# A two-block transformer kernel on one core: modulation sums turned outside the FFN loops, one sum for the final norm and the norm behind it, first chunks interleaved

## The chip, the cores and the metric

The kernel runs on one core of a Trainium2 chip. The time is the device time of one execution in microseconds (us), and before the change the median of three runs is 1651.37 us (1649.37 to 1656.2).

## What is computed

Two blocks work in a row on x, 256 tokens of width 1024, in f32. Each layer follows one pattern (shift, scale and gate come from the conditioning vector c):

```
mod = silu(c) @ mod_w[layer] + mod_b[layer]
h = rms_norm(x, norm_g) * (1 + sc1) + sh1
x = x + g1 * mixer(h)
h = rms_norm(x, norm_g) * (1 + sc2) + sh2
x = x + g2 * conv_ffn(h)
```

Block 1 has the mixers "state space + attention" (ab_in, glu, ab_out) and "conformer convolution" (cm_in, a gate, 31 causal taps per channel, a layer norm, silu, cm_out). It ends with `x = rms_norm(x, final_g)`. Block 2 has latent attention over x and a context ctx (dq, dkv, uq, ukv, 16 heads, mla_out) and a hyena mixer (hy_in, long filters, hy_out), and a final norm of its own. The FFN is 1024 to 2 x 2816 and back, with three taps per channel on the gate.

The change touches the place where the blocks meet. There the reference computes y = x * r * final_g with r = 1/sqrt(mean(x^2) + EPS), and then rms_norm(y, norm_mix_g_2).

## The kernel before

**Data.** Features lie on the 128 partitions, tokens in the free dimension: x is eight tiles of 128x256. Each f32 product is made as three products of rounded parts, hi*hi, lo*hi and hi*lo (`three`, L1845). So a chunk of weights (1 MB, 128x2048) costs 48 matmuls of 256 columns with eight feature tiles. Weights stream through three slots on SyncE's DMA queue; ScalarE makes w_hi (L650), VectorE w_lo (L1095). `chunk_ready` waits for both.

**Norms.** ScalarE squares x, two tiles at a time (L659). TensorE sums over the partitions with a matrix of ones (`norm_sum`, L1785: eight f32 matmuls, sixteen passes). ScalarE takes the root (L665), VectorE the reciprocal (`norm_rstd`, L1244). Then pair by pair of tiles: VectorE scales (L1262), ScalarE makes h_hi (L677), VectorE h_lo (L1272). `feature_chunk` and `up_gate` begin when the first pair is there, and go tile by tile of the output, each over all eight feature tiles. `final_norm` scales x in place (L1532).

**FFN.** `ffn` is a loop of five iterations of two steps on every engine. A step takes three chunks (gate, up, down); taps and silu run on VectorE and ScalarE (L1432).

**Modulation vectors.** mod_pe, for layer 0, goes over TensorE at the start. For both second layers the matrix mod_stream is multiplied on VectorE inside ffn0 and ffn1 (`mod_block`, L1123 to L1137, sixteen blocks of 384 columns each). `mod_turn` on TensorE (L1799, three matmuls of one column, six passes) sums a block's partitions, three times per iteration and once at the end. Products stand in a ring of three (`mod_acc`), for which `mod_block` waits. mod_later, for block 2's first layer, comes in 48 pieces of 512 KB into a ring of six slots, and TensorE multiplies them in rounds, `later(p)` (L2078), between the parts of the conformer stage; `later_copy` (ScalarE, L884) and `later_turn` (L2066) bring the results into columns.

**Conformer stage.** Eight chunks of cm_in, two a round. `conv_taps` (L2057) does 8 of the 31 taps on TensorE as products with diagonal matrices, VectorE the other 23 (L1574, 23 for each of the two tiles). The layer norm needs a sum of its own (L2094). The order is written out by hand:

```
for c in range(2 * p, 2 * p + 2):
    feature_chunk(Q["cm_in"] + c, ...)
if p:
    conv_taps(p - 1)
    later(p)
```

**Between the blocks.** final_norm(FINAL), then norm 6 of the scaled x, then the products dq and dkv with ctx's norm between them, then uq.

## Time and profile before

| | |
|---|---|
| median of three runs | 1651.37 us (1649.37 to 1656.2) |
| the profiled execution | 1647.83 us, its span 1646.0 us |
| mean granted TensorE clock | 0.956 |
| PE busy | 1495.4 us, 91% of the span |
| DVE (VectorE) busy | 1208.4 us, 73% |
| ACT (ScalarE) busy | 724.2 us, 44% |
| data read from HBM | 304.17 MB |

The span is one execution recorded on the core. PE is TensorE, SP SyncE, POOL GpSimd. The chain of waits follows the work that ended last back to the beginning: each row is a piece of an engine's work, or a transfer, that held up what came next. A row such as "PE bank L1845 x96" is 96 matmuls in one piece. The windows table gives what each engine was busy in a stretch of time, with the granted clock (1.00 is full).

### The profile page before, as it was taken

The numbers are of one execution on the slowest core, as the hardware profiler recorded it, in microseconds if no ns is written. First come the engines' busy times: TensorE is split into PE (matmuls) and PEld (weight loads), VectorE is DVE, ScalarE is ACT, GpSimd is POOL, SyncE is SP. The second block draws the span as 40 slices with busy tenths as digits, with TensorE's granted clock in tenths as the row PEclk, the third lists the DMA queues.
The fourth block names the chain that finished last, engine by engine and source line by source line (L and its number), as shares of the span: only waits on it lengthen the run. The fifth ranks groups of instructions, "written<-read, shape, count | busy, mean of one in ns | idle before, by whom it ended". The sixth has DMA issues, their size and how long they took to land.

```text
span 1646.0 us, 29088 instructions
## 1 busy us (share of the span) xinstructions
PE 1495.4 (91%) x11238; PEld 1348.5 (82%) x11238; DVE 1208.4 (73%) x1913; ACT 724.2 (44%) x949; POOL 52.1 (3%) x38
## 2 busy tenths in 40 slices
PE   4597898999989878999978899999999999899998
PEld 1484488999987668999967766889998877899997
DVE  7998647888879956888875545386666769466665
ACT  2222445444454235443444566354545442355443
POOL 2501200000000000000001000000000000000000
PEclk9698999999999989999979899999999999999999
DMA  8334827878845744878822400335554433245551
GB/s 350 128 103 166 298 99 301 316 297 309 325 163 197 275 193 184 347 294 304 301 111 103 128 14 1 130 106 202 178 185 170 164 119 103 77 149 176 182 182 51
DMA packets 55188, 307.85 MB, mean 187 GB/s; under 512 B 6631, under 2 KB 7688, under 8 KB 30984
## 3 DMA queue, kind: packets, MB, share of 16 engines
q1 hardware_dynamic: 53272, 302.40, 49.6%
q10 hardware_dynamic: 1840, 4.41, 0.9%
q8 instruction: 51, 0.84, 0.2%
q14 instruction: 25, 0.20, 0.0%
HBM read 304.17 MB, written 1.05 MB: 185 GB/s over the span
## 4 chain that ended last, share of the span: by engine, by line
PE 83%; DVE 9%; ACT 4%; issue 2%; DMA 2%; POOL 0%; ACTq 0%; DVEq 0%
PE bank L1845 66%; PE bank L1785 2%; PE bank L2192 2%; PE bank L2057 2%; PE bank L2042 2%; PE bank L2158 2%; DVE rstd L1244 2%; DMA arena<-in_mod_later 1%; DVE hf L1262 1%; DVE h_lo L1272 1%; PE bank L1799 1%; PE bank L2176 1%; PE bank L1811 1%; ACT w_hi L650 1%; PE bank L1896 1%
## 5 line engine op out<-in xcount | busy, mean ns | idle before, releaser
L1845 PE MATMUL bank<-h_hi,w_hi 128*128 128x256 f32 x2184 | 639.4, 293 | 64.1 <-DVE h_lo L1272 53.3
L1845 PE MATMUL bank<-h_lo,w_hi 128*128 128x256 f32 x2184 | 627.9, 287 | 0.0
L1845 PE MATMUL bank<-h_hi,w_lo 128*128 128x256 f32 x2184 | 627.4, 287 | 0.0
L1095 DVE TENSOR_TENSOR w_lo<-raw,w_hi 128x2048 fp32r<-128x2048 f32 x186 | 426.5, 2294 | 135.2 <-ACT w_hi L650 134.1
L1845 PEld LDWEIGHTS bank<-h_hi,w_hi 128*128 128x128 f32 x2184 | 428.5, 196 | 79.4 <-issue 65.8
L1845 PEld LDWEIGHTS bank<-h_lo,w_hi 128*128 128x128 f32 x2184 | 429.7, 197 | 1.1 <-issue 0.7
L1845 PEld LDWEIGHTS bank<-h_hi,w_lo 128*128 128x128 f32 x2184 | 428.9, 196 | 0.0
L650 ACT ACTIVATE w_hi<-raw 128x2048 fp32r<-128x2048 f32 x186 | 355.3, 1911 | 163.9 <-PE bank L1845 117.9
L1845 PE MATMUL bank<-a_hi,w_hi 128*128 128x256 f32 (+1 forms) x760 | 222.5, 293 | 9.9 <-DVE a_lo L1272 3.7
L1845 PE MATMUL bank<-a_lo,w_hi 128*128 128x256 f32 (+1 forms) x760 | 220.2, 290 | 0.0
L1845 PE MATMUL bank<-a_hi,w_lo 128*128 128x256 f32 (+1 forms) x760 | 220.0, 290 | 0.0
L1432 DVE SCALAR_TENSOR_TENSOR arena<-bank,par,arena 128x255 f32<-128x255 f32 (+1 forms) x264 | 109.1, 476 | 123.0 <-ACT arena L824 89.0
L1845 PEld LDWEIGHTS bank<-a_hi,w_hi 128*128 128x128 f32 x760 | 149.1, 196 | 12.7 <-DVE a_lo L1272 3.9
L1845 PEld LDWEIGHTS bank<-a_hi,w_lo 128*128 128x128 f32 x760 | 149.0, 196 | 0.8
L1845 PEld LDWEIGHTS bank<-a_lo,w_hi 128*128 128x128 f32 x760 | 149.0, 196 | 0.6
L824 ACT ACTIVATE arena<-bank,par 128x256 f32<-128x256 f32 x88 | 44.8, 560 | 170.5 <-PE bank L1845 170.5
L1129 DVE SCALAR_TENSOR_TENSOR arena<-arena,silu_c 128x384 f32<-128x384 f32 x192 | 104.3, 612 | 0.0
L1574 DVE SCALAR_TENSOR_TENSOR hf<-arena,par,hf 128x256 f32<-128x256 f32 x176 | 70.7, 480 | 1.0 <-DVE hf L1574 0.5
L1785 PE MATMUL bank<-sq,ones 128*128 128x256 f32 x208 | 53.8, 403 | 9.4 <-ACT sq L659 9.4
L842 ACT ACTIVATE a_hi<-arena 128x512 fp32r<-128x512 f32 x44 | 27.8, 631 | 67.5 <-DVE arena L1453 67.4
L1785 PEld LDWEIGHTS bank<-sq,ones 128*128 128x128 f32 x208 | 39.7, 201 | 17.3 <-ACT sq L659 12.0
L1244 DVE RECIPROCAL rstd<-std 128x256 f32<-128x256 f32 x15 | 26.3, 1752 | 37.2 <-ACT std L665 37.2
(265 smaller groups left out, 1486.6 us busy)
## 6 DMA issues: line engine op xcount, KB each, us to landing
raw<-in_stream SPq DMA_DIRECT2D x186, 1024.0 KB, 4.9
arena<-in_mod_stream SPq DMA_DIRECT2D x64, 768.0 KB, 6.4
arena<-in_mod_later SPq DMA_DIRECT2D x48, 512.0 KB, 6.8
raw<-in_mod_pe SPq DMA_DIRECT2D x36, 512.0 KB, 5.8
arena<-in_mod_pe SPq DMA_DIRECT2D x12, 512.0 KB, 12.6
sq<-in_bias SPq DMA_DIRECT2D x8, 256.0 KB, 7.0
x<-in_x_t ACTq DMA_DIRECT2D x1, 1024.0 KB, 9.2
arena<-in_ctx_t SPq DMA_DIRECT2D x1, 1024.0 KB, 4.9
```

The costliest lines, as they stand in the source:

```text
L650: nc.scalar.activation(w_hi[s][:], raw[s][:], ACT.Copy).then_inc(hi_done, 1)
L824: ins = nc.scalar.activation(gate_c[:, e, :], half(4, e), ACT.Identity, scale=par[:, bass.ds(wb[center] + 2 * s + e, 1)], bias=par[:, bass ...
L1095: nc.vector.tensor_tensor(w_lo[s][:], raw[s][:], w_hi[s][:].bitcast(F32), ALU.subtract).then_inc(lo_done, 1)
L1129: ins = nc.vector.scalar_tensor_tensor(acc[:, e, :], w, c, acc[:, e, :], ALU.mult, ALU.add)
L1244: nc.vector.reciprocal(rstd[:], std[:]).then_inc(sem("rstd_ready"), 1)
L1432: ins = nc.vector.scalar_tensor_tensor(o, src, par[:, bass.ds(w[tap] + 2 * s + e, 1)], o, ALU.mult, ALU.add)
L1574: chain.on(nc.vector.scalar_tensor_tensor(hf[:, k, :], padded[:, k, bass.ds(tap, T)], par[:, bass.ds(wt + k + DT * tap, 1)], hf[:, k, :], ...
L1785: ins = nc.tensor.matmul(bank[7][:, 0:T], ones[:], sq[:, k, :], start=(k == 0), stop=(k == 2 * pairs - 1))
L1845: ins = nc.tensor.matmul(out_, l, r, start=first and n == 0, stop=last and n == 2, **kw)
L2042: ins = nc.tensor.matmul(bank[2 * part + ft][:], dft[:, part, t, ft * P:(ft + 1) * P], sources[part][:, t, 512 * s_:512 * s_ + 512], start ...
L2057: nc.tensor.matmul(half(p % 3, e), diag[n], padded[:, 2 * p + e, t0:t0 + T], start=(t == 0), stop=(t == PE_TAPS - 1)).then_inc(sem("diag_u ...
L2158: nc.tensor.matmul(bank[u % 4][:], q_head[0:n, h, t * P:(t + 1) * P], k_head[0:n, h, :], start=True, stop=True)\
```

## The change

- mod_turn leaves the FFN loops. The sums of the sixteen blocks stay in `mod_keep`, so mod_block no longer waits for a ring. They are turned later: of ffn0's blocks 2 to 5 ahead of the last down product, 0 and 1 behind the sum of norm 2, 6 to 10 and 11 to 15 in the conformer stage; of ffn1's all between BOTH's sum and the k_pe turn. mod_out follows them.
- Ten taps on TensorE instead of eight (PE_TAPS).
- The pieces of mod_later per round are 0, 9, 9, 11, 11, 8 instead of 6, 8, 8, 8, 10, 8. The ring of six slots lies elsewhere, and its first six loads wait for all blocks of ffn0.
- FINAL and norm 6 become one norm, BOTH: the squares of x are scaled by both_q = sqrt(final_g^2 + EPS) and the sum takes EPS^2, the gain is the product of both gains. x itself is scaled after the uq product: four squares on ScalarE, a sum on TensorE and final_norm on VectorE; the addition of mla_out waits for it.
- Norm parts are made tile by tile, with three scaled ahead. The last two tiles of x are squared one by one.
- First chunks behind a norm take all their output tiles per pair of feature tiles (`feature_chunk` with staged, `first_up_gate`); their banks are opened with a product of zeros.
- `stay_awake(n)` issues n products of zeros (128x512, bf16) ahead of the first chunk: 13 in each FFN, 12 before cm_in, 20 before cm_out, 8 before dq, 17 before hy_in.

```diff
@@ -39,7 +39,7 @@
...
-PE_TAPS = 8
+PE_TAPS = 10
...
-        diag = [at(ffn0 + i * P, P) for i in range(2 * PE_TAPS)]
...
+        diag = [at(FREE - 2 * PE_TAPS * P + i * P, P) for i in range(2 * PE_TAPS)]
+        later_w = [at(i * PM_COLS, PM_COLS) for i in range(LATER_SLOTS)]
+        later_acc = [at(FREE + START_SLOTS * HALF + MOD_BLOCKS * MOD_COLS + (1 + i) * T, T) for i in range(2)]
+        MOD_KEEP = FREE + START_SLOTS * HALF
+        mod_keep = at(MOD_KEEP, MOD_BLOCKS * MOD_COLS)
...
         def later_pieces(p):
-            return range((0, 6, 14, 22, 30, 40)[p], (6, 14, 22, 30, 40, 48)[p])
+            return range((0, 0, 9, 18, 29, 40)[p], (0, 9, 18, 29, 40, 48)[p])
@@ -505,7 +507,9 @@
...
 
                 for m in range(m0, m1):
-                    if m >= LATER_SLOTS:
+                    if m < LATER_SLOTS:
+                        sp.wait_ge(sem("mod_used"), MOD_SLOTS + 2 * MOD_BLOCKS)
@@ -569,17 +573,15 @@
...
+            load_plain("cm_in", 0, 2)
             load_later(0, 6)
-            load_plain("cm_in", 0, 6)
-            load_later(6, 12)
-            load_plain("cm_in", 6, 7)
-            load_later(12, 18)
-            load_plain("cm_in", 7)
-            load_later(18, 20)
+            load_plain("cm_in", 2)
             load_plain("cm_out", 0, 1)
-            load_later(20, 27)
-            load_plain("cm_out", 1, 3)
-            load_later(27, 48)
+            load_later(6, 9)
+            load_plain("cm_out", 1, 2)
+            load_later(9, 15)
@@ -656,34 +659,48 @@
...
+            def square_tile(n, k):
+
+                by = both_q[:, k:k + 1] if n == BOTH else 1.0
+                nc.scalar.activation(sq[:, k, :], NORMS[n]["src"][:, k, :], ACT.Square, scale=by).then_inc(sem("sq_ready"), 1)
 
...
-                nc.scalar.activation(std[:], bank[7][:, 0:T], ACT.Sqrt, bias=eps[:, 0:1], scale=1.0 / NORMS[n]["width"])\
+                nc.scalar.activation(std[:], bank[7][:, 0:T], ACT.Sqrt, bias=(eps_2 if n == BOTH else eps)[:, 0:1], scale=1.0 / NORMS[n]["width"])\
...
-                    if ready is not None:
+                    if ready is not None and p == DT // 2 - 1:
+                        act.wait_ge(sem("x_half"), X_HALF[n])
+                        square_tile(n, DT - 2)
                         act.wait_ge(sem("x_ready"), ready + p + 1)
-                    square(n, p)
...
             norm_std(0)
+            act.wait_ge(sem("both_sum"), 1)
+            nc.scalar.activation(both_q[:], both_q[:], ACT.Sqrt).then_inc(sem("both_q_ready"), 1)
...
             ffn(1)
...
-
-            norm_x(6, 8)
...
+            for p in range(DT // 2):
+                square(FINAL, p)
+            norm_std(FINAL)
@@ -1100,17 +1126,16 @@
...
-                ring = mod_acc
-                acc = ring[b % len(ring)]
-                if b >= len(ring):
-                    dve.wait_ge(sem("mod_turned"), b - len(ring) + 1 + 3 * per)
+                part = mod_acc[b % len(mod_acc)]
+                k0 = b % MOD_BLOCKS * MOD_COLS
+                parts = [mod_keep[:, bass.ds(k0 + 3 * MOD_COLS * per, MOD_COLS)], part[:, 1, :]]
...
+            final_g = par[:, COL["final_g"]:COL["final_g"] + DT]
+            nc.vector.tensor_tensor(both_g[:], final_g, par[:, COL["norm_mix_g_2"]:COL["norm_mix_g_2"] + DT], ALU.mult)
+            link(nc.vector.tensor_tensor(both_q[:], final_g, final_g, ALU.mult))
+            nc.vector.tensor_scalar(both_q[:], both_q[:], EPS, None, ALU.add).then_inc(sem("both_sum"), 1)
@@ -1255,29 +1283,29 @@
...
+                tiles = v["kt"]
+
+                def scaled(k):
+                    nc.vector.scalar_tensor_tensor(hf[:, k, :], v["src"][:, k, :], gain(k), rstd[:], ALU.mult, ALU.mult)\
+                        .then_inc(sem("scaled"), 1)
+
...
+                    if k % 2:
+                        ins.then_inc(sem("h_ready"), 1)
+
+                for k in range(min(3, tiles)):
+                    scaled(k)
+                for k in range(tiles):
+                    lower(k)
+                    if k and k + 2 < tiles:
+                        scaled(k + 2)
@@ -1499,11 +1529,10 @@
...
-                if b0 is not None:
-                    mod_out((1, 4)[f], b0 + MOD_BLOCKS, ("mod_b", "mod_b_2")[f], 48)
...
+            mod_out(1, 6, "mod_b", 0, 18)
             norm(2)
...
                     add_taps(p - 1)
+                if p == 1:
+                    mod_out(1, 16, "mod_b", 18, 48, 2)
...
             ffn(1, 1, MB[4], 8)
-            final_norm(FINAL)
-
-
-            norm(6)
...
+            mod_out(4, 32, "mod_b_2")
@@ -1636,6 +1668,7 @@
...
+            final_norm(FINAL)
@@ -1673,6 +1706,7 @@
...
+            dve.wait_ge(sem("x_ready"), 12)
             add_to_x("mla_out", 3, 16)
...
             def norm_pair(n, p):
 
                 pairs = NORMS[n]["kt"] // 2
-                pe.wait_ge(sem("sq_ready"), SQ[n] + p + 1)
                 for k in range(2 * p, 2 * p + 2):
+                    pe.wait_ge(sem("sq_ready"), 2 * SQ[n] + k + 1)
                     ins = nc.tensor.matmul(bank[7][:, 0:T], ones[:], sq[:, k, :], start=(k == 0), stop=(k == 2 * pairs - 1))
                 if p == pairs - 1:
...
                     norm_pair(n, p)
 
-            def mod_turn(b, column, i=None, parts=2):
-
-                ring = mod_acc
-                pe.wait_ge(sem("mod_used"), MOD_SLOTS + 2 * b + 2 + (0 if i is None else 6 * i))
-                for n in range(3):
-                    for e in range(parts):
-                        ins = nc.tensor.matmul(bank[6][:, bass.ds(column + n, 1)], ring[b % len(ring)][:, e, n * P:(n + 1) * P], ones[:, 0:1],
-                                               start=(e == 0), stop=(e == parts - 1))
-                ins.then_inc(sem("mod_turned"), 1)
+            def stay_awake(n):
+
+                for i in range(n):
+                    nc.tensor.matmul(bank[i % 3][:], zeros[:, 0:P], zeros[:], start=True, stop=True)
+
+            def mod_turn(b0, blocks, dst=6):
+
+                for b in blocks:
+                    pe.wait_ge(sem("mod_used"), MOD_SLOTS + 2 * (b0 + b) + 2)
+                    for n in range(3 * b, 3 * b + 3):
+                        ins = nc.tensor.matmul(bank[dst][:, n:n + 1], mod_keep[:, n * P:(n + 1) * P], ones[:, 0:1], start=True, stop=True)
+                    ins.then_inc(sem("mod_turned"), 1)
 
...
+                    if late:
+                        pe.wait_ge(staged[0], staged[1][0])
+                    open_banks(fill, tiles // 2)
+                    for j, k in enumerate(order):
+                        if j % 2 == 0:
+                            pe.wait_ge(staged[0], staged[1][j // 2])
+                        for n in range(tiles):
+                            ins = three(half(4 + (fill + n // 2) % 2, n % 2), w_at(q, k, kt, n * P), (hh[:, k, :], hl[:, k, :]),
+                                        False, j == kt - 1, skip_group_check=True)
+                    ins.then_inc(chunk_done, 1)
+                    return
                 for n in range(tiles):
                     if n % 2 == 0 and fill + n // 2 >= 2:
                         pe.wait_ge(bank_free, fill + n // 2 - 1)
                     bb = 4 + (fill + n // 2) % 2
@@ -1981,24 +2035,45 @@
...
+            def ffn(f, b0=None):
...
+                stay_awake(13)
...
+                def first_up_gate(q, staged):
...
+                    def pair(j, n, p):
+                        for k in (2 * p, 2 * p + 1):
+                            ins = three(half(4 + j, n), w_at(q + j, k, DT, n * P), (h_hi[:, k, :], h_lo[:, k, :]), False, k == DT - 1,
+                                        skip_group_check=True)
+                        return ins
+
+                    for p in range(DT // 2):
+                        pe.wait_ge(staged[0], staged[1][p])
+                        pair(0, 0, p)
+                        ins = pair(0, 1, p)
+                        if p == DT // 2 - 1:
+                            ins.then_inc(chunk_done, 1)
+                        pair(1, 0, p)
+                    for p in range(DT // 2):
+                        ins = pair(1, 1, p)
+                    ins.then_inc(chunk_done, 1)
+
@@ -2016,21 +2091,17 @@
                             ins.then_inc(sem("down_done"), 1)
                     ins.then_inc(chunk_done, 1)
 
...
                         up_gate(s, q, i)
-                        if b0 is not None and e:
-                            mod_turn(b0 + 1, 9 * i + 3, i, parts=1)
                         down(s - 1, q + 2, i)
-                        if b0 is not None:
-                            mod_turn(b0 + 2 * e, 9 * i + 6 * e, i, parts=1)
+                if f == 0:
+                    mod_turn(b0, range(2, 6))
                 down(10, q0 + 32, last=True)
-                if b0 is not None:
-                    mod_turn(b0 + 15, 45, parts=1)
...
             norm_sum(2)
+            mod_turn(MB[1], (0, 1))
+            stay_awake(12)
...
                     conv_taps(p - 1)
+                if p < 2:
+                    mod_turn(MB[1], range(6 + 5 * p, 11 + 5 * p), 2)
+                if p:
...
             later(5)
             later_turn(5)
             norm_sum(LAYER_NORM)
+            stay_awake(20)
             projection("cm_out", 4, h_of(LAYER_NORM))
-            ffn(1, MB[4])
-            norm_sum(5)
-
-
-            norm_sum(6)
+            ffn(1)
+            norm_sum(BOTH)
+            mod_turn(MB[4], range(0, 3))
+            stay_awake(8)
             for c in range(2):
-                feature_chunk(Q["dq"] + c, FILL["dq"] + c, DT, h_hi, h_lo, staged=None if c else h_of(6))
+                feature_chunk(Q["dq"] + c, FILL["dq"] + c, DT, h_hi, h_lo, staged=None if c else h_of(BOTH))
                 if c == 0:
-                    norm_sum(7)
-            pe.wait_ge(sem("h_ready"), H[8])
+                    norm_sum(6)
+                    mod_turn(MB[4], range(3, 6))
+            mod_turn(MB[4], range(6, 11))
+            pe.wait_ge(sem("h_ready"), H[7])
...
                 if c == 0:
-                    norm_sum(8)
+                    norm_sum(7)
+                    mod_turn(MB[4], range(11, 14))
+            mod_turn(MB[4], range(14, 16))
...
-                    norm_sum(10)
+                    norm_sum(9)
+            norm_sum(FINAL)
...
             norm_sum(12)
+            stay_awake(17)
```

On TensorE, in the FFN loop (bank<-ones is mod_turn, a_hi,w_lo ends a down product, h_hi,w_hi begins gate or up), before:

```order
L1845 MATMUL bank<-a_hi,w_lo 128x256
L1796 REGISTER_ALU
L1799 ISA
L1799 MATMUL bank<-ones,arena 128x1
L1799 ISA
```

and after, at the end of the loop in ffn0:

```order
L1882 MATMUL bank<-a_hi,w_lo 128x256
L2097 REGISTER_ALU
L2097 COMPARE_AND_BRANCH
L1837 MATMUL bank<-ones,arena 128x1 x12
L1882 MATMUL bank<-a_hi,w_hi 128x256
```

No mod_turn is left inside; four blocks' stand behind it.

On TensorE, in the conformer stage, between the second and third pair of cm_in's chunks (L2057 and L2130 are taps, L2078 and L2151 pieces of mod_later, L2066 and L2139 later_turn), before:

```order
L1845 MATMUL bank<-h_hi,w_lo 128x256
L2057 MATMUL bank<-arena 128x256 x16
L2078 MATMUL bank<-arena 32x256 x8
L2066 MATMUL bank<-ident_sb,arena 128x4 x4
L2078 MATMUL bank<-arena 32x256 x24
L1845 MATMUL bank<-h_hi,w_hi 128x256
```

and after:

```order
L1882 MATMUL bank<-h_hi,w_lo 128x256
L2130 MATMUL bank<-arena 128x256 x20
L1837 MATMUL bank<-ones,arena 128x1 x15
L2151 MATMUL bank<-arena 32x256 x32
L2139 MATMUL bank<-ident_sb,arena 128x4 x4
L2151 MATMUL bank<-arena 32x256 x4
L1882 MATMUL bank<-h_hi,w_hi 128x256
```

Four tap products more, five blocks' turns, and nine pieces instead of eight.

On TensorE, at the end of the uq product (L2133 and L2214 turn q), before:

```order
L1845 MATMUL bank<-h_hi,w_lo 128x256
L2133 MATMUL bank<-arena 128x256 x4
L1845 MATMUL bank<-a_hi,w_hi 128x512
```

and after:

```order
L1882 MATMUL bank<-h_hi,w_lo 128x256
L1819 MATMUL bank<-sq,ones 128x256 x8
L2214 MATMUL bank<-arena 128x256 x4
L1882 MATMUL bank<-a_hi,w_hi 128x512
```

The sum for x's late scaling stands ahead of the turn.

## Rows read from the trace of the kernel before

**Rows 1.** Page: busy us (share) by engine; shares of the chain that ended last.
```profile
PE 1495.4 (91%) x11238; PEld 1348.5 (82%) x11238; DVE 1208.4 (73%) x1913; ACT 724.2 (44%) x949; POOL 52.1 (3%) x38
...
PE 83%; DVE 9%; ACT 4%; issue 2%; DMA 2%; POOL 0%; ACTq 0%; DVEq 0%
```

**Rows 2.** Windows: stretch, length, busy us by engine, PEclk, DMA share, GB/s.
```profile
339.25:375.77 36.52, 36.52 (x308) 36.52 (x308) 32.27 (x46) 15.86 (x15) 0.00 (x0) 1.00 0.78 302
...
468.00:600.00 132.00, 112.63 (x913) 92.85 (x913) 111.84 (x237) 52.83 (x107) 0.00 (x0) 0.95 0.61 232
```

**Rows 3.** Chain of one loop period in ffn0: start us, us, what.
```profile
356.62 0.56 PE bank L1799 x6
357.19 11.61 PE bank L1845 x96
368.80 0.56 PE bank L1799 x6
...
375.21 0.56 PE bank L1799 x6
```

**Rows 4.** Chain in the conv stage.
```profile
483.14 13.23 PE bank L1845 x96
496.38 6.91 PE bank L2057 x32
504.35 4.46 DMA arena<-in_mod_later
...
570.31 6.03 DMA arena<-in_mod_later
577.09 5.22 PE bank L2094 x16
```

**Rows 5.** Chain: first products behind norms.
```profile
599.51 13.78 PE bank L1845 x96
...
1278.01 14.40 PE bank L1845 x96
```

**Rows 6.** Timeline, end of ffn0: start, us, engine line, tile, xcount, idle before.
```profile
450.54 0.41 PE L1845 MATMUL bank<-a_hi,w_hi 128*128 128x256 f32 x1
...
453.10 3.26 DVE L1129 SCALAR_TENSOR_TENSOR arena<-arena,silu_c 128x384 f32<-128x384 f32 x6
```

**Rows 7.** Timeline, norm 1.
```profile
247.02 1.03 PE L1988 MATMUL bank<-zeros 128*128 128x512 bf16 x4
...
247.88 1.75 DVE L1244 RECIPROCAL rstd<-std 128x256 f32<-128x256 f32 x1 [2.48 <-ACT std L665]
...
252.56 0.55 PE L1845 MATMUL bank<-h_hi,w_hi 128*128 128x256 f32 x1 [4.51 <-DVE h_lo L1272]
```

**Rows 8.** Windows, the work of L2078 alone.
```profile
503.29:509.49 6.20, 4.00 (x64) 1.66 (x64) 1.00 0.70 254
...
552.78:560.03 7.25, 4.09 (x64) 1.60 (x64) 1.00 0.70 217
567.14:577.09 9.95, 5.56 (x80) 1.91 (x80) 0.99 0.83 298
```

**Rows 9.** Timeline of PE, conv stage.
```profile
483.14 0.36 PE L1845 MATMUL bank<-h_hi,w_hi 128*128 128x256 f32 x1 [1.93 <-DVE arena L1554]
...
575.23 0.64 PE L2078 MATMUL bank<-arena 128*32 128x256 f32 x8 [2.05 <-DMA arena<-in_mod_later]
```

**Rows 10.** Chain, the two norms between blocks.
```profile
844.90 1.77 DVE rstd L1244
...
855.08 1.76 DVE rstd L1244
859.75 8.00 PE bank L1845 x48
```

**Rows 11.** Timeline, end of the uq product.
```profile
933.71 1.91 ACT L650 ACTIVATE w_hi<-raw 128x2048 fp32r<-128x2048 f32 x1
...
933.87 2.50 PE L2133 MATMUL bank<-arena 128*128 128x256 f32 x8 [3.71 <-ACT arena L932]
```

More of the change, by code:

```diff
@@ L1853, in w_at, with feature_chunk @@
                 return w_hi[s][:, k * w + c0:k * w + c0 + n], w_lo[s][:, k * w + c0:k * w + c0 + n]
[L1855 removed]
+            def feature_chunk(q, fill, kt, hh, hl, staged=None, order=None, late=False):
                 chunk_ready(q)
@@ L1865, in feature_chunk, with open_banks @@
                     for j, k in enumerate(order):
-                        if staged is not None and n == 0 and j % 2 == 0:
-                            pe.wait_ge(staged[0], staged[1][j // 2])
                         ins = three(half(bb, n % 2), w_at(q, k, kt, n * P), (hh[:, k, :], hl[:, k, :]), j == 0, j == kt - 1)
                 ins.then_inc(chunk_done, 1)
+            def open_banks(fill, n):
+                for b in range(fill, fill + n):
+                    if b >= 2:
+                        pe.wait_ge(bank_free, b - 1)
+                    nc.tensor.matmul(bank[4 + b % 2][:], zeros[:, 0:P], zeros[:], start=True, stop=False, skip_group_check=True)
             def h_of(n):
```

166 lines of the change are left out of this document (88 added, 78 removed).

## The prediction

> **What bounds the kernel now.** I read the busy line first: TensorE works 91% of the span, VectorE 73% [rows 1]. The chain of waits confirms it, with 83% of the span on PE [rows 1]. So I went through the stages with the table by windows and asked of each what PE waits for. In an FFN loop PE is busy for 36.52 of 36.52 us at full clock, VectorE for 32.27 [rows 2]: PE sets the pace there, with 4.25 us in hand. The loop's chain shows that 3 x 0.56 us of a period are mod_turn, L1799, beside products of which 96 matmuls take 11.61, 0.12 each [rows 3]. In the conv stage (468 to 600) both are close to full, 112.63 and 111.84 of 132 us [rows 2]; the chain there is PE's, broken by waits for pieces of in_mod_later, of which the ring holds six [rows 4]. After each norm PE waits for VectorE's first pair of parts and then finds itself at the low clock: 96 matmuls take 13.2 to 14.4 us [rows 4, 5] against 11.61 in the loop [rows 3].
>
> The sum is against the profiled execution, 1647.8 us, which lies 3.5 below the median of the runs, 1651.4. I subtract from both. A measurement of this kernel can tell about 0.5%, 8.3 us, from no change.
>
> **FFN loops, blocks 0 and 1: -13.4.** The turns leave the loop. Each of the four periods between the first and the last one is worth 3 x 0.56 = 1.68 [rows 3]: 6.7 per FFN, 13.4 for two. The fifth gives nothing: there VectorE is last, with block 15's products (L1129 from 453.10, [rows 6]) and then the additions to x. Without its waits for the ring VectorE issues the same products, 32.27 of a period that becomes 34.84; the cover shrinks from 4.25 to 2.57 but holds. The DMA share of 0.78 in the period [rows 2] rises to 0.78 x 36.52/34.84 = 0.82, still below 1.
>
> **First chunks behind four FFN norms: -12.0.** Today the first matmul stands 2.93 us behind the reciprocal's end (247.88 + 1.75 to 252.56, [rows 7]), for a pair of tiles passes VectorE, ScalarE, VectorE at 0.89 us each. Taken per tile, with three scaled ahead, the pairs are there about 2.33, 4.05, 5.8 and 7.1 behind it (16 VectorE instructions of some 0.44). PE now takes 18 matmuls per pair (2.2 us at 0.12 each) instead of all pairs for one tile first. So pair p starts at 2.33, 4.5, 6.7 and 8.9, up1's last 24 matmuls follow at 11.1, and two chunks end 13.85 behind the reciprocal. Before: 2.93 + 11.6 + 2.0 for the low clock = 16.5. That is -2.65, and squaring the last tile alone gives 0.35: -3.0 each.
>
> The 2.0 of low clock depends on the zero matmuls (13 of 128x512) that fill PE's wait. Four such matmuls took 1.03 us from 247.02 on, and PE then waited until 252.56 [rows 7]. So 13 more take 3.4 of 4.5 us; with the first pair 0.6 earlier and the sum 0.35 earlier, some 4.3 remain: they fit.
>
> **Conv stage: +16.9.** All on PE, since VectorE's relief finds it no longer the later one:
> - Two more taps on PE: 8 passes a round of 0.216 (6.91 / 32, [rows 4]), so 1.73, times 4 = +6.9. VectorE loses 4 of its 46 L1574 instructions, some 0.41 each from start to start: -1.6 a round, which nobody waits for.
> - Ten turns (blocks 6 to 15) at 0.56 now stand between chunks: +5.6. Blocks 0 and 1 stand in the norm's gap, 2 to 5 before the last down product; in both places PE waits anyway.
> - Pieces of mod_later: the first six, which were multiplied in norm 2's gap, join the rounds, which become 9, 9, 11, 11, 8 instead of 8, 8, 8, 10, 8. With six slots, 3+3+5+5+2 = 18 pieces instead of 12 must be fetched while PE waits. The rows bound the price: the pass itself, 0.52 (4.1/8, [rows 8]), and the worst wait with its passes, 2.05 + 0.64 = 2.7 [rows 9]. The round with 10 pieces lasted 9.95, two with 8 6.20 and 7.25 [rows 8]: (9.95 - 6.7) / 2 = 1.6 for one more. I take 1.5, since the first of these rounds gives less: 6.20 less six resident pieces at 0.5 is 3.2 for two. 6 x 1.5 = +9.0; the bounds are +3 and +16.
> - VectorE takes block 0 and 1's sums (mod_out) ahead of norm 2, and so waits for two turns on PE: +1.1. Interleaved first chunk and per-tile parts: -2.3 (a chunk of 48 now ends 7.1 + 12 x 0.12 = 8.6 behind the reciprocal, before 10.9). PE's wait of 1.93 ahead of the second chunk (483.14, [rows 9]) gets covered by the turns: -1.9. The second chunk pair then keeps its clock, 13.23 to 11.7: -1.5.
>
> DMA: what the trace shows for a piece of 512 KB is 4.5 to 6.0 us of wait in a round's chain [rows 4]. The Trainium skill's DMA: Bandwidth & Descriptors, section Anatomy of one DMA, gives 2.0 us plus bytes over 436 GB/s, an estimate of 3.2 us here; by it a fetched piece would be worth about 0.9, and the sum some 4 us lower. The trace disagrees for a queue with other pieces in flight, so I keep the rows.
>
> **cm_out: -2.2.** Its first 96 matmuls took 13.78 [rows 5]; at full clock 11.6. Its parts come from other code (L1592, L1596), which the change leaves.
>
> **The norm BOTH: -5.4.** Before, reciprocal (844.90), scaling of x, squares and their sum, a second reciprocal, parts, first matmul 859.75, 48 matmuls in 8.00 [rows 10]. Now one reciprocal, at about 844.65, ends 846.4, and a staged chunk ends 8.6 behind it, at 855.0 instead of 859.75 + 8.00 = 867.75: -12.7. Of that 1.5 comes back, as ctx's norm and w_lo of dq, which stood in the freed time, follow. dkv starts 11.2 earlier. Against it stand +1.7 (blocks 11 to 13 ahead of dkv's second chunk) and +5.7 for the late scaling: a sum of sixteen passes (16 x 0.216 = 3.5) behind four squares of ScalarE that cannot begin before 935.6, behind w_hi at 933.71, while PE was free to go on at 933.87 + 2.50 [rows 11]: 935.6 + 4 x 0.55 + the sum's tail against 936.4, about 5.7. dkv's first 96 matmuls, which begin behind such a wait too, keep their clock, taken like the others: -1.6. The scaling of x itself, eight VectorE instructions at some 0.41, falls beside the heads, where PE is busy; it must be done before mla_out. Sum: -11.2 + 1.7 + 5.7 - 1.6 = -5.4. POOL's zeroing of the head tiles waits for the last turn, well before the heads need it: nothing.
>
> **Rest: -3.2.** hy_in: same as an FFN norm, -2.9 (its 96 matmuls took 14.40, [rows 5]). hy_out -1.0, mla_out +0.2. Extra VectorE work at the start, for both_g and both_q: +0.5.
>
> **Sum:** -13.4 - 12.0 + 16.9 - 2.2 - 5.4 - 3.2 = -19.3. The profiled execution becomes 1628.5, the median **1632**.
>
> **Rivals.**
> A. *The zero matmuls don't hold the clock.* What I count for it is 4 x 2.0 + 2.2 + 1.6 + 2.8, about 14. For: even inside a running FFN the clock was low at the last product, 0.41 us a matmul [rows 6], as behind the norms, although PE had worked until shortly before; so some work in a gap may not do. Against: the loop never falls. Without it 1632 + 14 = 1646, within no change. By the rows 13 zero matmuls cost 3.4 at 0.26 each; at half the clock they would cost 6.8, and run past the first pair by about 2 us a norm, six times. The Trainium skill, TensorE: Matmul & The Clock Gate, section on the back-to-back issue gap, gives 426.7 ns for 512 columns cold, 215.7 warm: 5.5 us cold, an estimate, so a smaller overrun of the same kind. Chance 0.13.
> B. *VectorE, not PE, sets the conv stage.* Then 4 x 1.6 = 6.5 is gained there and PE's extra work is hidden: -19.3 - 16.9 - 6.5 = -42.7, 1608.7. For: both engines' busy times are within 1 us of each other [rows 2]. Against: the chain lies on PE through all rounds [rows 4]. Chance 0.12.
> C. *The other side: the ring of six starves.* Place: the rounds of 9 and 11 pieces. Each of 18 fetched pieces costs the full 2.7: 48.6 instead of 18 + 9, +21.6, and after each of five longer waits PE falls to the low clock, 1.6 each, +8. Together +30: 1662. It is slower than before as a whole only from +28 on. Against: the worst wait occurred once [rows 9]. Chance 0.05.
> D. *VectorE becomes the FFN loop's bound.* 32.27 leaves 2.57 in 34.84, which small waits for ScalarE's w_hi could use up. Half the gain lost gives 1639, all of it 1645. Chance 0.08.
>
> **How the numbers follow.** Forecast 0.60, A 0.13, B 0.12, D 0.08, C 0.05, other 0.02. The forecast's own range, from the bounds of the pieces and +-4 on the clock, is 1624 to 1641. To hold 8 in 10 the whole range goes from B's 1608 to A's and D's 1646; C and what lies beyond are left out. Faster by over 0.5% means below 1643.1: the forecast 0.56 (its tail is lost), B 0.12, most of D and a third of A, 0.10: 0.78. Slower: C and a little: 0.06. The same: 0.16.
>
> **What would show it.** An FFN period near 34.8 with no L1799 counterpart in the chain; two chunks ending 13.9 behind the reciprocal; one reciprocal fewer in a row at 845 and dkv at about 869 on the old scale; the conv stage 17 longer, with longer DMA waits in the rounds of 11; full clock behind norms. The forecast is wrong if the conv stage grows by less than 8 (B) or more than 30 (C), if a period stays above 35.6 (D), or if 96 matmuls behind a norm still take over 13 us (A).

## The result

The changed kernel takes 1643.39 us (median of eleven runs, 1640.9 to 1646.87) against 1651.34 us before. The ratio is 0.9949, with a 95% interval of 0.9938 to 0.9960. So it is faster by 8.0 us, by the medians just under the 0.5% (8.3 us) that I called no change, and not by 19.

The change's profiled execution took 1644.33 us, 0.9 above its median, while the one of before lay 3.5 below its own. So the two traces differ by only 3.4 us of span. The page of the changed kernel (busy line, and the chain's shares):

```profile
PE 1529.7 (93%) x11399; PEld 1363.5 (83%) x11399; DVE 1200.4 (73%) x1902; ACT 733.6 (45%) x977; POOL 52.1 (3%) x38
...
PE 80%; DVE 11%; ACT 3%; issue 3%; DMA 3%; POOL 0%; DVEq 0%; ACTq 0%
```

PE is busy 34 us longer, and DMA has gone from 2% of the chain to 3%. The reciprocals on VectorE mark where a stage begins in both traces, so their distances give the stages:

| stage, reciprocal to reciprocal | before | change | difference | forecast |
|---|---|---|---|---|
| start to norm 1 | 247.9 | 245.3 | -2.6 | +0.5 |
| ffn0 (norm 1 to norm 2) | 214.9 | 205.1 | -9.8 | -9.7 |
| conformer stage (norm 2 to layer norm) | 131.2 | 163.8 | +32.6 | +16.9 |
| cm_out (to norm 4) | 36.0 | 33.7 | -2.3 | -2.2 |
| ffn1 (to the first norm between blocks) | 214.9 | 204.1 | -10.8 | -9.7 |
| latent attention (to norm 11) | 225.5 | 223.3 | -2.2 | -5.2 |
| ffn2 | 202.9 | 203.5 | +0.5 | -3.0 |
| hyena | 163.3 | 158.1 | -5.2 | -3.9 |
| ffn3 | 201.9 | 198.2 | -3.6 | -3.0 |

The forecast's +1.1 for mod_out stands ahead of norm 2's reciprocal, so by this cut it belongs to ffn0 (-8.6) and not to the conformer stage (+15.8); the rows are left as forecast. The conformer stage alone holds 15.7 us of the miss. Here is the chain of waits of the changed kernel there (start us, us, what), behind the chain of ffn0's loop, the counterpart to [rows 3, 4]:

```profile
249.16 167.31 PE bank L1882 x1392
...
454.26 12.08 PE bank L1882 x96
466.34 4.01 PE bank L1837 x30
470.35 13.90 PE bank L1882 x96
484.25 8.63 PE bank L2130 x40
492.88 3.32 PE bank L1837 x30
496.21 2.76 PE bank L2151 x24
498.98 7.20 DMA arena<-in_mod_later
507.31 12.72 PE bank L1882 x96
520.03 8.64 PE bank L2130 x40
528.67 2.33 PE bank L2151 x41
531.00 6.02 DMA arena<-in_mod_later
...
561.88 8.07 DMA arena<-in_mod_later
571.08 10.50 PE bank L2130 x40
...
593.28 6.15 PE bank L2170 x16
...
607.94 5.62 PE bank L1819 x16
```

ffn0 is now one piece of 1392 matmuls: 0.120 us each, no turn in it. In the conformer stage the chain of the first four rounds holds a transfer of a piece of mod_later that took 6.0 to 8.1 us, where it was 4.5 to 6.0; only the last is as before (4.46). Such a row is the time from issue to landing. PE multiplies other pieces meanwhile: in the first of these rounds it is idle for 3.4 of 11.1 us, in the third for 4.2 of 11.6. The work behind such a wait is longer too: 40 passes of taps in 10.50 instead of 8.64, the sum of 16 in 5.62 instead of 3.57. The table by windows shows the clock of three rounds, the counterpart of [rows 8] (stretch, length, busy us by engine, PEclk, DMA share, GB/s):

```profile
496.21:507.31 11.10, 7.69 (x81) 3.43 (x81) 10.85 (x28) 0.38 (x1) 0.00 (x0) 0.81 0.75 266
...
559.45:571.08 11.63, 7.41 (x93) 2.86 (x93) 10.74 (x27) 0.79 (x3) 0.00 (x0) 0.85 0.87 329
...
581.58:593.28 11.70, 7.10 (x94) 2.71 (x93) 0.69 (x1) 0.38 (x1) 0.00 (x0) 0.92 0.87 332
```

Before, the pieces' products ran at 1.00 or 0.99 [rows 8]. And in the timeline of PE, the five fetched pieces of the third round (last brackets: idle before):

```profile
563.76 0.64 PE L2151 MATMUL bank<-arena 128*32 128x256 f32 x8 [0.47 <-DMA arena<-in_mod_later]
565.02 0.64 PE L2151 MATMUL bank<-arena 128*32 128x256 f32 x8 [0.62 <-DMA arena<-in_mod_later]
566.43 0.64 PE L2151 MATMUL bank<-arena 128*32 128x256 f32 x8 [0.78 <-DMA arena<-in_mod_later]
567.71 1.08 PE L2151 MATMUL bank<-arena 128*32 128x256 f32 x8 [0.63 <-DMA arena<-in_mod_later]
570.00 1.08 PE L2151 MATMUL bank<-arena 128*32 128x256 f32 x8 [1.21 <-DMA arena<-in_mod_later]
```

They follow each other at 1.3 to 2.3 us, and the last two run at the low clock (1.08 instead of 0.64), after a stretch in which PE stood idle about half the time. The taps and the two sums that took longer ran at a granted clock of 0.84, 0.59 and 0.64.

### The profile page after: what moved, and what is told of

It is laid out like the page before. It is cut to its first block, busy times and chain, and to the rows that moved or that the text cites. A ratio compares the mean times of both kernels' runs of the same rounds, so it can differ in the third digit from the quotient of the medians.

```text
span 1642.6 us, 29301 instructions
## 1 busy us (share of the span) xinstructions
PE 1529.7 (93%) x11399; PEld 1363.5 (83%) x11399; DVE 1200.4 (73%) x1902; ACT 733.6 (45%) x977; POOL 52.1 (3%) x38
## 4 chain that ended last, share of the span: by engine, by line
PE 80%; DVE 11%; ACT 3%; issue 3%; DMA 3%; POOL 0%; DVEq 0%; ACTq 0%
PE bank L1882 62%; PE bank L1819 2%; PE bank L2130 2%; DMA arena<-in_mod_later 2%; PE bank L2273 2%; PE bank L2113 2%; PE bank L2239 1%; DVE hf L1289 1%; DVE w_lo L1121 1%; DVE rstd L1272 1%; DVE h_lo L1298 1%; ACT w_hi L653 1%; PE bank L2151 1%; PE bank L1837 1%; PE bank L2257 1%
## 5 line engine op out<-in xcount | busy, mean ns | idle before, releaser
L1882 PE MATMUL bank<-h_hi,w_hi 128*128 128x256 f32 x2184 | 632.2, 289 | 24.3 <-DVE h_lo L1298 19.3
L1154 DVE SCALAR_TENSOR_TENSOR arena<-arena,silu_c 128x384 f32 (+1 forms) x192 | 104.3, 613 | 0.0
L1819 PE MATMUL bank<-sq,ones 128*128 128x256 f32 x208 | 58.2, 429 | 8.7 <-ACT sq L666 7.5
L1606 DVE SCALAR_TENSOR_TENSOR hf<-arena,par,hf 128x256 f32<-128x256 f32 x160 | 64.3, 478 | 0.8 <-DVE hf L1606 0.5
L688 ACT ACTIVATE h_hi<-hf,mod 128x256 fp32r<-128x256 f32 x64 | 31.1, 506 | 53.2 <-DVE hf L1289 53.2
```

The costliest lines, as they stand in the source:

```text
L688: ins = nc.scalar.activation(v["parts"][0][:, k, :], hf[:, k, :], ACT.Identity, bias=mod[:, v["l"], v["sh"] + k:v["sh"] + k + 1])
L1154: ins = nc.vector.scalar_tensor_tensor(parts[e], w, c, parts[e], ALU.mult, ALU.add)
L1606: chain.on(nc.vector.scalar_tensor_tensor(hf[:, k, :], padded[:, k, bass.ds(tap, T)], par[:, bass.ds(wt + k + DT * tap, 1)], hf[:, k, :], ...
L1819: ins = nc.tensor.matmul(bank[7][:, 0:T], ones[:], sq[:, k, :], start=(k == 0), stop=(k == 2 * pairs - 1))
L1882: ins = nc.tensor.matmul(out_, l, r, start=first and n == 0, stop=last and n == 2, **kw)
```

## The experiments

The median of a run is given beside that of the changed kernel, 1643.4; "stage" is the conformer stage, 163.8 there. Where that stage's code was untouched (e5, e6, e9) it took 160.3 to 163.6, so a difference of 3 us there is within what one kernel shows. Other stages of unchanged code repeated within 0.1 or lay 1 to 2 apart, the start up to 3.8. The kernel before, run again beside each group of experiments, had medians of 1652.2 to 1654.3, up to 3 us above the 1651.3 here: medians of different groups are no surer than that, and small effects are read from the stages.

The runs with nine or twelve slots (e2, e7, e8, e10, e11, e13, e15) also move loads of cm_in and cm_out among those of the pieces in SyncE's queue. No run has that order with six slots, so what is said of the slots holds for both together.

### 1. The turns at the FFN's end (e1_turns)

```diff
-                if f == 0:
-                    mod_turn(b0, range(2, 6))
+                if b0 is not None:
+                    mod_turn(b0, range(*((2, 6), (2, 8))[f]))
                 down(10, q0 + 32, last=True)
+                if b0 is not None:
+                    mod_turn(b0, range(*((6, 15), (8, 15))[f]))
...
-                if p < 2:
-                    mod_turn(MB[1], range(6 + 5 * p, 11 + 5 * p), 2)
```

> The changed kernel with the turns at other places: of ffn0 blocks 6 to 14 and of ffn1 2 to 14 stand around the last down product, where PE waits for VectorE, and 0, 1, 15 behind the norm's sum; none stands between chunks. Theory (the turns between chunks cost their passes, 4.0 and 3.3 us in the conformer stage and 7 us around dkv, and leave PE at the low clock for the product behind them, 2.3, 1.5 and 1.5 us): 11 us less in the conformer stage and 7 less around dkv, 18 in all, a time near 1626. Rival 1 (only 0.56 a turn, as the forecast had it, and no clock loss): 5.6 and 5.6, near 1632. Rival 2 (the turns only fill waits for pieces of mod_later): under 3, near 1641.

Measured 1658.28 us, 15 slower. The stage fell only to 161.8, which is within what the untouched stage shows: rival 2, in the stage. The ten turns there had filled waits for pieces: the five rounds grew from 52.4 to 56.5 as they left. Around dkv the theory had 7 less, and latent attention went from 223.3 to 221.9 only. The loss came at the new place, +9.2 in ffn0 and +7.7 in ffn1. The chain at ffn0's end:

```profile
437.80 7.48 PE bank L1880 x48
445.28 7.46 PE bank L1835 x54
452.74 5.34 PE bank L1817 x16
458.08 1.92 PE bank L1835 x18
```

Nine turns took 7.46, 0.83 each at a granted clock of 0.78, behind a down product that had only just ended. I had taken PE for idle there; it is idle before the down product, not behind it. A turn took 0.56 in the loop, which runs at full clock, and 0.62 to 0.83 in the other places.

### 2. Twelve slots for mod_later (e2_ring12)

Beside e1's edit:

```diff
-LATER_SLOTS = 6
+LATER_SLOTS = 12
...
-        later_w = [at(i * PM_COLS, PM_COLS) for i in range(LATER_SLOTS)]
+        later_w = [at((0 if i < 6 else MOD_KEEP - 6 * PM_COLS) + i * PM_COLS, PM_COLS) for i in range(LATER_SLOTS)]
```

> As e1_turns, and the ring for mod_later has twelve slots instead of six (the other six lie where the products of the blocks stood, and wait for the turns). Theory (a fetched piece can't be asked for before a slot is free, so the ring of six starves PE; its waits of 0.5 to 1.6 us for each of 18 pieces and the low clock behind them are the excess): the rounds of 9 to 11 pieces shrink from 8.5 to 11.7 us to about 6, and the conformer stage by another 20 to 25 us. Rival (the transfers themselves are the limit, 0.75 to 0.87 of the DMA engines in these rounds): the waits stay and it gives under 6.

Measured 1622.53 us. Against e1_turns the stage fell by 37.2, to 124.6. The DMA wait has left the chain:

```profile
505.47 11.70 PE bank L1880 x96
517.17 8.64 PE bank L2130 x40
525.81 3.20 PE bank L2151 x56
...
530.53 1.00 PE bank L2151 x16
531.53 11.71 PE bank L1880 x96
```

and the table by windows for all of the stage behind the second pair of chunks has full clock:

```profile
491.12:582.00 90.88, 88.34 (x785) 71.35 (x785) 79.74 (x176) 36.08 (x82) 0.00 (x0) 1.00 0.68 261
```

The five rounds take 29.0 us in all (5.7, 5.7, 6.1, 6.1, 5.3) against 52.4 in the changed kernel and 56.5 in e1_turns. So the transfers are not the limit, since the same bytes now come beside other work; when they can be asked for is, by the slots and by the order of the queue. The other 10 of the 37 are clock: the same chunks, taps and sums took 98.8 us in e1_turns and 89.2 here.

### 3. Eight taps on TensorE (e3_taps8)

```diff
-PE_TAPS = 10
+PE_TAPS = 8
```

> The changed kernel with 8 taps on TensorE as before. Theory (PE sets the conformer stage): 8 f32 passes a round less, 7 to 9 us faster. Rival (VectorE sets it, or PE then only waits longer for pieces of mod_later, which arrive no earlier): within 2 us of the changed kernel, or slower by up to 6.

Measured 1633.2 us, 10 faster, with the stage at 152.3, 11.5 less. The traces give the passes themselves 6.9 of it; the rest is rounds, turns and sums that took less (the squares' sum 3.57 for 5.62), of which up to 3 us can be the stage's own spread. The two more taps thus made the change worse by their 32 passes at least; in the pair e7_ring9 and e8_ring9_taps8 they cost 10 again.

### 4. No products of zeros (e4_no_zeros)

```diff
             def stay_awake(n):
-                for i in range(n):
-                    nc.tensor.matmul(bank[i % 3][:], zeros[:, 0:P], zeros[:], start=True, stop=True)
+                return
```

> The changed kernel without its 96 products of zeros ahead of first chunks (stay_awake). Theory (they hold TensorE's clock): the 96 matmuls behind a norm go from 11.5 to 12.1 us back to 13.2 to 14.4, about 14 us slower over seven norms. Rival (the clock is held by the interleaved order of the first chunks, whose work starts earlier): under 3 us slower.

Measured 1650.76 us, 7.4 slower, by the two traces 5.7: about half the theory's 14. cm_out's stage lost 2.4 (its first 96 matmuls 14.16 instead of 11.78, see below), latent attention 2.4 and ffn3 1.6. ffn0, ffn1 and hyena lost 1.1 to 1.5 each, but they differ by as much between runs with the zeros in (205.1 or 206.8, 204.1 or 205.5, 158.1 or 159.0); ffn2 gained 1.5 and the conformer stage 3.8, in the same way. The chain of e4_no_zeros:

```profile
617.83 14.16 PE bank L1881 x96
...
1285.61 13.19 PE bank L1881 x96
```

and of the changed kernel:

```profile
619.57 11.78 PE bank L1882 x96
...
1282.65 12.08 PE bank L1882 x96
```

Without the zeros these 96 matmuls ran at a granted clock of 0.81 and 0.88, with them at 1.00. So zeros hold the clock, at 1 to 2.4 us a norm. Where chunks are interleaved the 96 took 13.1 to 13.2 without zeros, against 13.8 and 14.4 before, so the new order seems to have shortened the low stretch by itself; no run changes the order alone.

### 5. Nine slots, the turns where the change has them (e7_ring9, e8_ring9_taps8)

```diff
-LATER_SLOTS = 6
+LATER_SLOTS = 9
...
+        later_w = [at(a, PM_COLS) for a in [i * PM_COLS for i in range(6)] + [12032, MOD_KEEP, MOD_KEEP + PM_COLS]]
...
-            load_plain("cm_in", 2)
-            load_plain("cm_out", 0, 1)
+            load_plain("cm_in", 2, 5)
             load_later(6, 9)
```

The two slots in mod_keep wait for the first six turns. e8_ring9_taps8 has PE_TAPS = 8 as well.

> The changed kernel, turns where the change has them, and nine slots instead of six for pieces of mod_later (three in free or freed parts of the arena). Theory (starvation of the ring is what the forecast missed; in e2 the conformer stage took 124.6 us instead of 163.8): the waits for pieces nearly vanish, and with them the cover of the ten turns, which now cost their 7.3 us and some low clock. Stage about 136, whole near 1616. Rival (the stage needs the twelve slots, since a round has 9 to 11 pieces and its transfers can only start in the round): stage above 150, whole above 1630.

> As e7_ring9, with 8 taps on TensorE. Theory (PE sets the stage): 8 passes a round less, 6.9 us faster than e7_ring9. Rival (with the waits gone VectorE sets it, whose 46 tap instructions a round were even with PE before): under 2 us, or slower.

e7_ring9 measured 1622.5 us, the stage 140.4, 4 more than the theory had: the last pieces still wait at its end. e8_ring9_taps8 measured 1612.4 us, stage 128.4. PE still sets it, so fewer taps on PE gain 10, more than the 6.9 of their passes: the chunk pair behind the turns (11.61 for 13.92) and the last sum (3.57 for 5.21) kept their clock too. With the ring fixed the ten turns are no longer covered (3.24 or more for five, in the chain of both). That is what e2_ring12 avoids, which pays for them at the FFN's end instead, to the same sum.

### 6. The two norms apart again (e9_unmerged)

```diff
-            norm(BOTH)
+            final_norm(FINAL)
+            norm(6)
...
-            final_norm(FINAL)
             lo_upto(Q["ukv"] + 4)
...
-            norm_sum(BOTH)
+            norm_sum(FINAL)
+            norm_sum(6)
```

> The changed kernel with the two norms between the blocks apart again: x scaled by the final norm first, then squared, summed and normed once more; nothing left to scale behind the uq product. All else is as in the changed kernel. Theory (the second sum and reciprocal cost about 10.5 us, of which the late scaling takes 5.7 back): 4 to 6 us slower than the changed kernel, with some 10 more before dkv and 6 less at the uq product. Rival (the late scaling costs as much as it saves): within 1.5 us of it.

Measured 1648.12 us, 4.7 slower, with latent attention at 226.9 instead of 223.3; dkv begins 35.6 behind the first reciprocal instead of 25.1. The theory holds: the merged norm is worth 3.6 us by its stage and 4.7 by the medians.

### 7. The kernel before with twelve slots (e10_before_ring12)

```diff
-        later_w = [at(LATER + i * PM_COLS, PM_COLS) for i in range(LATER_SLOTS)]
+        later_w = [at((LATER if i < 6 else -6 * PM_COLS) + i * PM_COLS, PM_COLS) for i in range(LATER_SLOTS)]
...
+                    elif m >= 6:
+                        sp.wait_ge(sem("mod_turned"), MOD_BLOCKS)
```

> The kernel before with twelve slots for pieces of mod_later (the six new ones where the blocks' weights and products stood, free once all are turned) and its rounds of 6, 8, 8, 8, 10, 8 as they were. Theory (the ring of six cost the kernel before too: 12 fetched pieces at 0.5 to 2 us of wait, and the low clock at the mean's sum): 10 to 14 us faster than before, near 1640. Rival (there VectorE was even with PE, so PE's waits were mostly hidden): under 4 us.

Measured 1645.19 us against 1652.17 of before in the same runs, ratio 0.9952 (0.9941 to 0.9964): 7 faster, between the theory (10 to 14) and the rival (under 4). The stage fell from 131.2 to 127.8 only, and the two traces differ by 0.7. The header of its chain from 460 to 600 says why:

```profile
by line: DVE hf L1575 26.8%; issue 20.9%; PE bank L1846 13.9%; DVE w_lo L1096 4.9%; DVEq L1143 4.4%; DVEq L1575 4.3%; PE bank L1786 3.2%; PE bank L2079 2.6%; DVE rstd L1245 2.5%; PE bank L2095 2.5%; DVE hf L1593 1.8%; DVE arena L1555 1.7%; 
```

With no wait for pieces left in it, VectorE's tap instructions (L1575) hold the largest share of the chain: before the change both engines and the ring were nearly even.

### 8. Turns and rounds as before, twelve and six slots (e11_loop_turns, e14_ring6)

Both keep the changed kernel's taps, interleaved chunks, merged norm and zeros (4 instead of 12 before cm_in and 13 instead of 8 before dq, where turns have left or pieces come back).

```diff
+                        if b0 is not None and e:
+                            mod_turn(b0 + 1, 9 * i + 3, i, parts=1)
                         down(s - 1, q + 2, i)
+                        if b0 is not None:
+                            mod_turn(b0 + 2 * e, 9 * i + 6 * e, i, parts=1)
...
-            return range((0, 0, 9, 18, 29, 40)[p], (0, 9, 18, 29, 40, 48)[p])
+            return range((0, 6, 14, 22, 30, 40)[p], (6, 14, 22, 30, 40, 48)[p])
```

> The changed kernel with the turns back inside the FFN loops, as before the change (ring of products, mod_out at each FFN's end), the rounds of mod_later as before (6, 8, 8, 8, 10, 8, the first six in norm 2's gap), and twelve slots for its pieces. Theory (a turn costs 0.56 us in the loop at full clock, and 0.65 to 0.83 with low clock behind it anywhere else, so taking the turns out gained nothing once nothing else hides them): against e2_ring12 the FFN stages lose the 9 and 8 us that its turns cost at their ends and gain back 7 each as loop work: 4 to 10 us faster than e2_ring12 and e7_ring9, near 1614. Rival (the loops' gain of 6.7 each was real and is lost here): 1629 or more.

> e11_loop_turns with six slots for mod_later instead of twelve: turns in the loops, rounds and loads of mod_later as before the change, 10 taps, interleaved chunks, zeros, merged norm. It tells what of the conformer stage's 32.6 us more comes from the new rounds and the later first loads, and what from the taps. Theory (12 fetched pieces as before, so the stage is before's 131.2 with 6.9 for the taps, less 2 to 5 for the first chunks): 133 to 137 us in the stage, whole near 1633; the other 27 to 30 us of the changed kernel's stage come from turns, rounds and what follows on them. Rival (longer PE work between the rounds, or the taps, upset the ring by themselves): stage 145 or more, whole above 1643.

e11_loop_turns measured 1621.86 us: as e2_ring12 and e7_ring9, not 4 to 10 faster. Its stage is 123.3, but ffn0 takes 215.2, the 214.9 of before and not 3 less: its first turn waits for VectorE's sum of products, PE stands idle for 1.2 us, and the chunks behind it find the low clock (the chain, with the later pair at full clock for comparison):

```profile
282.29 0.82 PE bank L1839 x6
283.11 13.09 PE bank L1885 x96
...
321.11 11.61 PE bank L1885 x96
```

So what the first chunks gain is given back at the first turn. Moving the turns out is thus worth about 10 us per FFN (215.2 to 205.1, 214.1 to 204.1), more than their passes, and costs it again elsewhere: with the ring mended, turns in the loop, at the FFN's end or between chunks all give 1622 (e11_loop_turns and e2_ring12 with twelve slots, e7_ring9 with nine).

e14_ring6 measured 1634.89 us, 8.5 faster than the changed kernel, stage 134.9. Its chain shows a round as it was before:

```profile
501.42 1.05 PE bank L2158 x16
502.49 4.51 DMA arena<-in_mod_later
507.04 0.64 PE bank L2158 x8
507.68 11.71 PE bank L1886 x96
519.39 8.64 PE bank L2137 x40
```

Ten taps, zeros and interleaving make the stage 3.7 longer than before (134.9 to 131.2). The other 28.9 come with the moved turns: their own passes, and the rounds of 9 to 11 pieces that this change pairs with them, because its six slots are free only when the last block is done.

### 9. The late scaling and ffn2 (e5_final_late, e6_swap), and all together (e13_best10, e15_best8)

```diff
-            lo_upto(Q["mla_out"] + 6)
             filter_angle(0)
+            lo_upto(Q["mla_out"] + 6)
...
-            norm_sum(FINAL)
             pe.wait_ge(bank_free, FILL["uq"] + 6)
...
+            norm_sum(FINAL)
             pe.wait_ge(bank_free, FILL["ukv"] + 16)
...
+                if h == 1:
+                    norm_rstd(FINAL)
+                if 2 <= h < 2 + DT:
+                    final_tile(FINAL, h - 2)
```

The first hunk is e6_swap, the others e5_final_late, which also moves the squares and the root on ScalarE. e13_best10 adds both to e11_loop_turns, e15_best8 adds both to e8_ring9_taps8.

> The changed kernel with the final norm's squares and sum behind the ukv products instead of behind uq, its reciprocal and the eight scalings one by one beside the heads. Theory (at the uq product the sum costs a wait for four squares and sixteen passes at low clock, 5.7 to 6.3 us; behind ukv only its passes at full clock, 3.5): 2 to 4 us faster than the changed kernel. Rival (VectorE and ScalarE are needed by the heads, and the moved work delays them by as much): within 1 us, or slower.

> The changed kernel with one line moved on VectorE ahead of ffn2: filter_angle(0) before the w_lo it stood behind. Theory (in ffn2 the interleaved chunks end earlier than that chain of small operations, so the taps behind it hold PE up by 1.7 us at 1091.5, and the low clock follows; that took the 3 us expected there): ffn2's stage shortens by 2 to 4 us. Rival (something else holds ffn2, the w_lo itself): no difference beyond 1 us.

e5_final_late measured 1641.95 us, latent attention 220.9 instead of 223.3: 2.4, as expected. e6_swap measured 1642.1 us, ffn2 200.2 instead of 203.5: 3.2, as expected. In runs where ffn2 was as in the changed kernel it took 202.0 or 203.5, so 1.8 of it is sure; e13_best10 and e15_best8 have 200.2 again. The medians moved by 1.4 and 1.3; the intervals of their ratios, 0.9907 to 0.9944 and 0.9917 to 0.9960, overlap that of the changed kernel, so the stages carry this, not the medians.

> e11_loop_turns with the moves of e5_final_late and e6_swap. Theory (they act in stages of their own): their gains add to e11_loop_turns, 4 to 7 us faster than it, near 1608. Rival (ffn2 begins earlier, and takes back what the other gave): as e11_loop_turns within 2 us.

> e8_ring9_taps8 with the moves of e5_final_late and e6_swap. Theory (their gains of 2 to 5 us lie in stages of their own): 5 us under e8_ring9_taps8's 1612.4, near 1607. Rival (the gain in ffn2 is given back): within 2 us of it.

e13_best10 measured 1616.77 us, 5.1 under e11_loop_turns. e15_best8 measured **1607.63 us**, ratio 0.9719 (0.9696 to 0.9743): 46 us faster than before and 36 faster than the changed kernel's median. It is the changed kernel with nine slots and their order of loads, eight taps on TensorE, the final norm's sum behind ukv, and filter_angle(0) first.

## Why the prediction was wrong

**The step that failed is "pieces of mod_later", +9.0 with bounds of +3 and +16.** The same five rounds took 36.1 us in e14_ring6 (6.3, 6.2, 6.1, 9.8, 7.7) and 52.4 in the changed kernel: +16.3 for six more pieces, 2.7 each, the upper bound and not 1.5. I priced a fetched piece by what two or four of them cost in a round that was else short, and I read the chain's 4.5 to 6.0 us as PE's wait, which is the time of one transfer. But slots become free only as pieces are used, so a third and fifth fetched piece comes at the pace of the transfers (1.3 us and more, timeline above) and PE works half the time. The second mistake is coupled to it: in that half-idle work the clock falls. The forecast credited 1.5 of clock in this stage; against e14_ring6 the chunk pairs lost 2.6 (51.4 to 48.8), taps 1.7, the mean's sum 0.8 and the squares' sum 2.1. That is 7.2 the other way. (Some 2 of it can be chance: in e5_final_late, with the same code there, the squares' sum took 3.57.) It was rival C's mechanism: its 8 for the clock nearly whole, of its 21.6 for the pieces a third (16.3 against the forecast's 9.0). The stage's 32.6 also passes the 30 that the prediction gave as C's sign. C had 0.05.

Turns: 7.3 us of passes, not 5.6, as their x30 rows show (0.134 and 0.111 a pass, where the loop's six take 0.56). But in e1_turns taking them away gave 2.0, within the stage's spread: beside a starving ring they were nearly free. The forecast added what overlapped. In an account of stages in the chain 7.3 + 16.3 + 7.2, less the gap of 1.9 that they cover, is 28.9, the difference of the two stages.

**Right.** The FFN loops: a period of 34.56 us (VectorE's a_lo returns every 34.55 to 34.57), forecast as 34.84, and -9.8 and -10.8 for -9.7 (for ffn0 -8.6, with mod_out). Both parts came out: four periods give -7.8 for -6.7, and two chunks end 13.8 behind the reciprocal for 13.85. But they aren't separate: with the turns left in the loop the -3.0 of the first chunks did not show in ffn0 (e11_loop_turns). cm_out -2.3 for -2.2, ffn3 -3.6 for -3.0, first matmul 2.15 behind the reciprocal's end (1.76 from 245.25, to 249.16) for 2.33. PE sets the conformer stage (e3_taps8, e8_ring9_taps8), which speaks against rival B. Of the kernel before this was less sure than it looked, since the ring kept PE late there: without waits VectorE's taps hold the largest share of the chain (e10_before_ring12). Rival A is half true: the clock was kept, but zeros were worth 6 to 7 of the 14 that I put on them (e4_no_zeros). D did not occur.

**Latent attention,** -2.2 for -5.2. dkv begins 25.1 behind the first reciprocal instead of 35.7, 10.7 earlier (11.2 in the forecast). From dkv's start on the stage is 8.5 longer, where the forecast had 6.0. The chain holds more turns than the one group I priced (blocks 11 to 13), and dkv found the low clock:

```profile
866.03 1.90 PE bank L1837 x18
867.94 5.87 PE bank L1882 x48
873.80 3.24 PE bank L1837 x30
877.04 13.11 PE bank L1882 x96
890.16 1.73 PE bank L1819 x8
891.89 1.90 PE bank L1837 x18
...
934.46 6.27 PE bank L1819 x16
```

The -1.6 that I credited to dkv's clock is not there (13.11 for 13.28 before, granted 0.87), and the late sum took 6.27 at a granted clock of 0.59 instead of 3.5; the total of that term, 5.7, was about right, as e5_final_late gave back 2.4 by moving it.

**ffn2,** +0.5 for -3.0. The forecast took four FFN norms as alike. In ffn2 a chain of small operations for the hyena filter stands on VectorE ahead of the taps (timeline of the changed kernel):

```profile
1085.07 2.29 DVE L1121 TENSOR_TENSOR w_lo<-raw,w_hi 128x2048 fp32r<-128x2048 f32 x1 [1.32 <-ACT w_hi L653]
1087.28 0.53 DVE L1444 TENSOR_SCALAR arena<-bank,hy_cols 64x256 f32<-64x256 f32 x1
...
1091.51 1.66 DVE L1462 SCALAR_TENSOR_TENSOR arena<-bank,par,arena 128x255 f32<-128x255 f32 x4 [1.39 <-ACT arena L849]
```

PE's matmul behind those taps began only at 1093.22, after 1.71 us of idle time, and the granted clock of the next 11.8 us was 0.86. Before, the first chunks ended later and PE had no such gap. With that chain moved ahead (e6_swap) the gap is gone and the stage is 3.2 shorter.

**The start,** -2.6 for +0.5: the glu chunks, behind whose interleaving I put nothing, took 11.51 for 96 matmuls instead of 13.19, in e7_ring9 and e8_ring9_taps8 too, and the chain reached them 0.7 earlier. But the fourteen runs with this start took 244.6 to 248.3, and the two with the start of before 247.9 and 246.2, so of the -2.6 at most these 1.7 are shown; the rest can be chance.

Of the DMA rule weighed in the prediction (the Trainium skill, DMA: Bandwidth & Descriptors, Anatomy of one DMA), the slope agrees with the rows: 512 KB over 436 GB/s is 1.2 us, and four fetched pieces follow each other at 1.26 to 1.41. The section's heading names the gpsimd path, while these loads are SyncE's; they took 3.4 us at least from issue to landing and 6.9 in the median, against the estimate of 3.2. What a fetched piece cost PE was 2.7, three times the 0.9 that I worked out by it.

## What to carry to other kernels

Before moving work to where engines look idle, count what the new place's buffers can hold: a ring that is refilled only as it is emptied turns a longer round into waits of transfer time, and the low clock behind them added nearly half as much again (7.2 to 16.3). Small products that sum partitions were cheap only beside a wait; once there was none, it made no difference which busy place they stood in. And when a stage waits on a ring, mend the ring first: which engine bounds it can be read only after that.

## What had not been expected

- Three more slots (nine for six), with the loads reordered for them, were worth 21 us, 1643.4 to 1622.5, more than all of the change's own gain.
- Turns (128x1 products) did not always hold the clock, though PE was busy all along. The same thirty passes behind the first chunks of cm_in took 4.01 us at a granted clock of 0.78 in the changed kernel, and the 96 matmuls behind them 13.90 at 0.82; e6, e7 and e9 show the same. In e5, e8 and e15 they took 3.24 at 1.00, and the 96 matmuls 11.61. Between the changed kernel and e5 no code of that stage differs. What decides it stays open.
- One identical stage came in two lengths: ffn2 at 202.0 or 203.5, ffn0 at 205.1 or 206.8 (hyena behind the shorter ffn2 at 159.0 for 158.1, in most runs). The profiles don't say why; a stage's difference under 2 us needs more than one trace.
